# Seven products instead of eight in half the depth of 18 of the 24 tile pairs of an input projection, in split float32

## The reference, cut to what matters

```python
xn = _rmsnorm(x, n1g)
z = xn @ w_in                                  # (576, 2048) @ (2048, 6152)
bg, cg, xt, q, k, v, o, ig, fg = jnp.split(z, _SPLIT_IDX, axis=-1)
u = cg * xt
pad = jnp.concatenate([conv_buf, u], axis=1)
conv = sum(pad[:, j:j + S] * conv_w[j] for j in range(CONV_W))
y_conv = _rmsnorm(bg * conv, conv_g)
h, C1, n1, m1 = _mlstm_chunked(q, k, v, li, lf, C0, n0, m0)
y_ml = jax.nn.sigmoid(o) * _rmsnorm(h, ml_g)
x = x + jnp.concatenate([y_conv, y_ml], axis=-1) @ w_out
hn = _rmsnorm(x, n2g)
x = x + (jax.nn.silu(hn @ wg) * (hn @ wu)) @ wd
```

## Time and profile before

| | us |
|---|---|
| median of 3 runs (lowest to highest) | 2466.73 (2466.65 to 2467.93) |
| the profiled execution | 2466.16 |
| its span, first to last instruction | 2464.4 |
| TensorE busy in the span | 2444.1 |
| VectorE busy in the span | 1760.1 |
| ScalarE busy in the span | 894.7 |

### The profile page before, as it was taken

One profiled execution on the slowest core, in us unless ns is written; L12 is line 12 of the kernel. 1 busy time (PEld: TensorE's weight loads), 2 busy tenths in 40 slices (PEclk: granted clock), 3 DMA queues, 4 the chain that ended last, 5 costly groups with the idle time before them and its releaser, 6 DMA issues.

```text
span 2464.4 us, 44130 instructions
## 1 busy us (share of the span) xinstructions
PE 2444.1 (99%) x17544; PEld 2380.3 (97%) x17544; DVE 1760.1 (71%) x2453; ACT 894.7 (36%) x1235; POOL 48.3 (2%) x79
## 2 busy tenths in 40 slices
PE   9999999999999999999999999999999999999998
PEld 8999999999999998999999999999999999999886
DVE  7576585675687678778877877787777866866535
ACT  5222222122233335443344344434344533544313
POOL 0010000000000000000000000000000000000100
PEclk9999999999999999999999999999999999999999
DMA  5443343343336575443443434434334655745822
GB/s 132 118 132 89 114 120 95 85 134 95 105 101 184 174 210 174 120 120 111 128 119 104 128 111 121 118 112 121 117 101 116 246 153 160 264 129 144 286 73 77
DMA packets 459979, 329.09 MB, mean 134 GB/s; under 512 B 14407, under 2 KB 429283, under 8 KB 457425
## 3 DMA queue, kind: packets, MB, share of 16 engines
q1 hardware_dynamic: 403704, 250.29, 34.7%
q10 hardware_dynamic: 51448, 58.42, 7.6%
q0 software_dynamic: 4640, 17.73, 2.1%
HBM read 268.02 MB, written 58.37 MB: 132 GB/s over the span
## 4 chain that ended last, share of the span: by engine, by line
PE 60%; DVE 1%; ACT 0%; issue 0%; DVEq 0%; ACTq 0%
PE ps L838 17%; PE ps L842 17%; PE ps L840 17%; PE ps L853 2%; PE ps L956 2%; PE ps L958 2%; PE ps L960 2%; PE ps L983 0%; PE ps L964 0%; PE ps L965 0%; DVE oplo L2153 0%; PE ps L865 0%; DVE gw_ring L2140 0%; DVE dwlo L2409 0%; ACT ophi L1314 0%
## 5 line engine op out<-in xcount | busy, mean ns | idle before, releaser
L838 PE MATMUL ps<-ophi,gw_ring 128*128 128x288 f32 x3208 | 950.4, 296 | 5.0 <-DVE up L2197 3.5
L840 PE MATMUL ps<-oplo,gw_ring 128*128 128x288 f32 x3208 | 947.0, 295 | 0.0
L842 PE MATMUL ps<-ophi,gw_ring 128*128 128x288 f32 x3208 | 945.4, 295 | 0.0
L838 PEld LDWEIGHTS ps<-ophi,gw_ring 128*128 128x128 f32 x3208 | 602.4, 188 | 6.1 <-DVE up L2197 3.9
L842 PEld LDWEIGHTS ps<-ophi,gw_ring 128*128 128x128 f32 x3208 | 604.9, 189 | 0.0
L840 PEld LDWEIGHTS ps<-oplo,gw_ring 128*128 128x128 f32 x3208 | 603.1, 188 | 0.1
L1039 ACT ACTIVATE whi<-wraw 128x512 fp32r<-128x512 f32 x256 | 160.6, 632 | 576.2 <-PE ps L608 369.1
L605 PE MATMUL ps<-xhi,whi 128*128 128x288 f32 x1536 | 332.3, 298 | 0.5 <-DVE wlo L1612 0.5
L608 PE MATMUL ps<-xhi,wlo 128*128 128x288 f32 x1536 | 328.6, 296 | 0.0
L605 PE MATMUL ps<-xlo,whi 128*128 128x288 f32 x1536 | 328.5, 295 | 0.0
L2140 DVE TENSOR_TENSOR gw_ring<-graw_a,gw_ring 128x1024 fp32r<-128x1024 f32 x191 | 233.6, 1223 | 111.4 <-ACT gw_ring L1292 110.8
(11 more groups left out here) (339 smaller groups left out, 2669.9 us busy)
## 6 DMA issues: line engine op xcount, KB each, us to landing
wraw<-in_w_in_dram SPq DMA_DIRECT2D x96, 512.0 KB, 3.9
graw_a<-in_w_ffn_gate_dram SPq DMA_DIRECT2D x59, 512.0 KB, 3.7
graw_a<-in_w_ffn_up_dram SPq DMA_DIRECT2D x59, 512.0 KB, 4.7
graw_a<-in_w_ffn_down_dram SPq DMA_DIRECT2D x42, 512.0 KB, 5.8
wraw<-in_w_out_dram SPq DMA_DIRECT2D x32, 512.0 KB, 4.0
opraw<-hop SPq DMA_DIRECT2D x14, 1152.0 KB, 11.5
graw_b<-in_w_ffn_gate_dram SPq DMA_DIRECT2D x29, 512.0 KB, 3.8
graw_b<-in_w_ffn_up_dram SPq DMA_DIRECT2D x29, 512.0 KB, 4.7
```

What stands on the lines that cost most here:

```text
L838: pe.matmul(out, gw_ring[:, slot, 0, k, :], ophi[p][:, k, :], start=start and k == 0, stop=False, skip_group_check=True)
L840: pe.matmul(out, gw_ring[:, slot, 0, k, :], oplo[p][:, k, :], start=False, stop=False, skip_group_check=True)
L842: mm = pe.matmul(out, gw_ring[:, slot, 1, k, :], ophi[p][:, k, :], start=False, stop=k == GK - 1, skip_group_check=True)
```

## The change

Two column tiles make a pair p, six pairs a head. In 18 of the 24 pairs (head 0: pairs 3 to 5; heads 1 and 2: all; head 3: pairs 0 to 2) the k blocks 0 to 7 are computed with the seven products of the Winograd form of Strassen's method: rows of the 2 by 2 blocks are the two column tiles, the inner index is k quarter 0 or 1, the columns are the token halves. The k blocks 8 to 15 stay direct and are added into the same banks. A pair is then 11 slots of weights: seven `p` (12 matmuls each) and four `d` (24 each), 180 matmuls in place of 192. All other pairs stay direct, in slots `t` of a quarter.

Three of the seven factors of x that are sums replace or join blocks of x and are made once in head 0 (`operand_sums`, `operand_raw`, `operand_low` on VectorE, `operand_high` on ScalarE, 128 by 1152 each); the quarter of x that they replace is loaded back for head 3. The gains of the `d` and `t` slots are multiplied in by VectorE; those of the four quarters under the seven products by ScalarE (`quad_gain`, four instructions of 128 by 128). The four sums of weights are VectorE's (`weight_total`). Raw weights come in 256 KB pieces into six places. A head's outputs go to HBM (`mix_d`) and come back for the output projection, which frees the room for the new tiles. The loops over heads on SyncE, ScalarE and VectorE are written out.

```diff
+    HALF_K = ("p1", "p0", "d0", "p2", "p3", "d1", "p4", "p5", "d2", "p6", "d3")
+    seven = lambda h, p: (h == 0 and p >= 3) or 0 < h < H - 1 or (h == H - 1 and p < 3)
+            order = (("a21", "p4"), ("a22", "p6"), ("a11", "p4"), ("d0", "d0"), ("a12", "p5"), ("d1", "d1"),
+                     ("d2", "d2"), ("d3", "d3"))
...
+            def half_product(n, name, bank, start, stop, ready=None):
...
+                for k in range(4):
+                    pe.matmul(out, whi[:, w, k, :], hi[:, k, :], start=start and k == 0, stop=False, skip_group_check=True)
+                    pe.matmul(out, whi[:, w, k, :], lo[:, k, :], start=False, stop=False, skip_group_check=True)
+                    mm = pe.matmul(out, wlo[:, w, k, :], hi[:, k, :], start=False, stop=stop and k == 3,
+                                   skip_group_check=True)
+                mm.then_inc(w_used, 1)
...
+            def seven_pair(h, p, early=None, mid=None):
...
+                before = (tile_read, i + 1) if not seven(*PLAN[PLAN.index((h, p)) - 1]) else (a_read, 2 * g)
...
+                half_product(n, "p1", "c", True, False)
+                half_product(n + 1, "p0", "a", True, False, before)
+                direct_part(n + 2, 2, (("b", 0, True, False, None), ("c", 1, False, False, (copy_q, 3 * g + 1))))
+                if early:
+                    early()
...
+                half_product(n + 3, "p2", "a", False, False, (copy_q, 3 * g + 2))
+                half_product(n + 4, "p3", "b", False, False)
+                direct_part(n + 5, 3, (("b", 0, False, True, None), ("c", 1, False, False, None)))
+                if mid:
+                    mid()
...
+                half_product(n + 6, "p4", "a", False, False, (copy_q, 3 * g + 3))
+                half_product(n + 7, "p5", "c", False, True)
+                direct_part(n + 8, 2, (("d", 1, True, False, (tile_read, i + 1)), ("a", 0, False, False, (a_read, 2 * g + 1))))
...
+                half_product(n + 9, "p6", "a", False, False)
+                direct_part(n + 10, 3, (("a", 0, False, True, None), ("d", 1, False, True, None)))
...
+                if seven(h, 3):
+                    seven_pair(h, 3, mid=numerator)
+                    seven_pair(h, 4, early=sample_states)
+                    head_squares()
+                    seven_pair(h, 5)
+                    seven_pair(h + 1, 0)
...
+            def quad_gain(h, p, name):
...
+                for k in range(4):
+                    ins = act.mul(raw_slot[j][:, k, :], raw_slot[j][:, k, :], vecs[:, col + k:col + k + 1])
+                ins.then_inc(quad_ok, 1)
...
+                n = FIRST[h, p] + s + 4
...
+                hi(n)
+                h, p, name = SLOTS[n]
+                if seven(h, p) and name in ("p1", "d0"):
+                    quad_gain(h, p, dict(p1="a11", d0="a12")[name])
+                elif name in ("p6", "d3", "t12", "t13"):
+                    nxt = PLAN[PLAN.index((h, p)) + 1:][:1]
+                    if nxt and seven(*nxt[0]):
+                        quad_gain(*nxt[0], "a21" if name in ("p6", "t12") else "a22")
...
+            def ahead(n):
+
+                if n < N_IN:
+                    h, p, s = SLOTS[n]
+                    if by_vector(s):
+                        gain(n)
+                    elif s in SUMS:
+                        weight_total(h, p, s)
+
+            def split(n):
+
+                ahead(n + 1)
+                low(n)
...
+                def c11(h, p, out):
+                    g = SEVENTH[h, p]
+                    slot_done(slot_of(h, p, "d1"))
+                    dve.wait_ge(copy_q, 3 * g + 2)
+                    link(tt(p1s[:], ps[:, 2, 0:HT], p1s[:], ALU.add))
+                    return out(p1s[:], 0)
...
+                def c21_c22(h, p, out):
+                    g = SEVENTH[h, p]
+                    slot_done(slot_of(h, p, "d3"))
+                    out(ps[:, 0, 0:HT], 0).then_inc(a_read, 1)
+                    dve.wait_ge(a_read, 2 * g + 1)
+                    link(tt(p5s[:], ps[:, 1, 0:HT], p5s[:], ALU.add))
+                    evac(out(p5s[:], 1))
...
+                    step(h, 5, 0)
+                    rms_of_h()
+                    step(h, 5, 1)
+                    rms_rest()
+                    sum_squares(0)
+                    steps(h, 5, 2, 3, 4, 5)
+                    link(c11(h, 5, by_tile(cg, cg)))
+                    conv_prompt(0, HT)
+                    u3(h, 5)
+                    step(h, 5, 6)
+                    mixed_heads()
+                    step(h, 5, 7)
+                    c12(h, 5, by_tile(cg, cg))
+                    dve.wait_ge(tile_read, i + (10 + 2))
+                    conv_prompt(HT, T)
+                    step(h, 5, 8)
+                    conv_sample(1)
+                    conv_scaled(1)
+                    step(h, 5, 9)
+                    c21_c22(h, 5, by_tile(own_conv(1), cv))
+                    step(h, 5, 10)
```

More of the change, by code:

```diff
@@ L380, in _, with load_out @@
         def _(sp):
[L381 to L390, removed]
+            def load_out(m, p, before):
+                for half in range(2):
+                    sp.wait_ge(lo_done, before(half))
+                    sp.sem_inc(halves_free, 1)
+                    sp.dma_start(wraw[:, half, 0:8, :], w_out_k[:, ds(MIX_K[8 * half], 8), ds(m * P + p * (GK * P), P)]).then_inc(raw_in[half], 16)
             xp = x_prompt.rearrange("l t d -> (l t) d")
@@ L399, in _, with load_quarter @@
                 sp.dma_start(xtok[last:XTW, XT - 1, c], xs[:, c]).then_inc(tok_in[b], 16)
[L401 to L410, removed]
+            def load_quarter(h, p, name, j, free):
+                if free:
+                    sp.wait_ge(lo_done, free)
+                k0 = 4 * quarter_k(h, p, name)
+                sp.dma_start(raw_slot[j], w_in_k[:, k0:k0 + 4, ds(column_of(h, p, name), P)]).then_inc(g_raw[j], 16)
             def small_inputs():
@@ new lines, in gemm @@
+                for n in range(KT):
+                    w = ring(n0 + n // 4)
+                    if n % 4 == 0:
+                        pe.wait_ge(lo_done, n0 + n // 4 + 1)
+                    if n in between:
+                        between[n]()
+                    if ready:
+                        ready(n)
+                    k, (out, first, last) = ks[n], where[n]
+                    for moving in (hi, lo):
+                        for a in halves:
+                            pe.matmul(out[:, a, :], whi[:, w, n % 4, :], moving[:, 2 * k + a, :],
+                                      start=first and moving is hi, stop=False)
+                    for a in halves:
+                        mm = pe.matmul(out[:, a, :], wlo[:, w, n % 4, :], hi[:, 2 * k + a, :],
+                                       start=False, stop=last)
+                    if n % 4 == 3:
+                        mm.then_inc(w_used, 1)
@@ L2011, in round_of_head @@
[L2011 removed]
+                step(h, 5, 7)
+                sum_squares(1)
+                rows_from_psum()
             def mix_low(n):
@@ L2024, in rows_from_psum @@
                 dve.tensor_copy(conv_rows[:], side(BLK_B, DC)[0:2 + 2 * NB]).then_inc(rows_out, 1)
[L2026 to L2031 removed]
+            for h in range(H):
+                round_of_head(h)
             for n in range(10, KT):
```

1244 lines of the change are left out of this document (795 added, 449 removed).

## The result

| us | before | after |
|---|---|---|
| median of 12 runs each, taken side by side (lowest to highest) | 2466.88 (2466.06 to 2468.39) | 2471.93 (2469.71 to 2475.36) |
| the profiled execution | 2466.16 | 2471.64 |
| its span | 2464.4 | 2469.8 |
| mean granted clock of TensorE in it | 0.998 | 0.995 |

The ratio is 1.0021, with a 95% interval of 1.0013 to 1.0028. The forecast was 2463.5, a gain of 0.13%; the time came out 8.4 us above it, inside the range of 2443 to 2481.

The account below looks back on a forecast made before the run. TensorE, busy for 99% of the span, was taken as the bound. 2466.16 less 28.8 for removed matmuls plus 25.5 of stalls gave 2462.9; with 0.57 for the median of runs, 2463.5 us, range 2443 to 2481.

Parts of the forecast that it names:

- pairs 0, 1, 2: Light pairs of a head: VectorE's 15 us and at most 3.5 us of head pieces fit, no stall.
- `p0` behind pair 3: TensorE waits for VectorE's `c21` to free bank 0 after pair 3: 1.0 us a head.
- `d2` of pair 4: VectorE splits slot 8 late in pair 4: 1.4 us, then 0.9 to 1.0 at its second half; 2.4 us lost.
- the transfers, at `d3` of pair 4: ScalarE's `quad_gain` waits for a weight piece in pair 4, delaying `d3`: 1 us a head, bounds 0 and 4.
- `p0` behind pair 5: VectorE frees bank 0 at 29.7 us, TensorE wants it at 25.6 after the heaviest pair: 4.1 us lost a head.
- the sum: Stalls of 8.5 us a head over three heads, 25.5 us, set against 28.8 us of removed matmuls: 2462.9 us.
- the clock falls: TensorE's clock drops after the stall behind pair 5, thrice: 5.3 us more, 2469 us; chance 0.18.
- The gain comes through: VectorE's pieces fit in pairs 3 to 5, only 0 to 2 us a head lost: 2441 us; chance 0.24.
- ScalarE stands in line for a transfer: `quad_gain` waits ahead of `d3`'s rounding in pairs 4 and 5: 7.2 us a head more, 2485 us; chance 0.18.

Follow-up runs that it names:

- experiment 1: Changed kernel with VectorE's mixed outputs made in pair 0 of the next head instead of pair 5: 2457.1 us, ratio to before 0.9961.
- 12: Changed kernel with mixed outputs in next pair 0, spills tied to pair 5's `c12`, `sample_update` behind pair 4's `u3`, three gains a head by ScalarE: 2443.9 us.
- experiment 5: Changed kernel with 36 TensorE transposes of a constant filling each wait behind pair 5, computation unchanged: 2467.6 us, ratio to before 1.0001.
- experiment 7: Changed kernel with mixed outputs in the next pair 0 and GpSimd's spread and spill waiting for them: 2470.6 us, ratio to before 1.0014.
- experiment 3: Changed kernel with GpSimd's spread and spill after the next head's mixed outputs, in pair 5 instead of pair 4: 2467.0 us, ratio to before 0.9998.

## Why the prediction was wrong

**The working that held.** 216 matmuls at 0.133 us went. The steps beside what they measured, each for a head:

| step | forecast | measured in heads 0, 1, 2 |
|---|---|---|
| pairs 0, 1, 2 | no stall | none |
| `p0` behind pair 3 | 1.0 | 1.07 |
| `d2` of pair 4 | 1.4 + 1.0 | 1.87 + 0.57 |
| the transfers, at `d3` of pair 4 | 1.0 | 0, 1.12, 1.11 |
| `p0` behind pair 5 | 4.1 | 3.91, 3.95, 3.97 |
| second half of `d2` in pair 5 | none | 0, 0.33, 0.33 |

The three heads sum to 25.5 forecast and 25.2 measured. A sum of instructions in one queue, with its slots' ends beside it, foresaw VectorE's waits to within half a microsecond; the term for the transfers was 1.0 off in head 0. Most instructions cost what their nearest rows did. VectorE's timeline of after ahead of the end of the long wait shows the piece that experiment 1 moved, and the read that frees the bank:

```profile
373.28 0.81 DVE L2307 SCALAR_TENSOR_TENSOR v0f<-v0f,gml,rh 128x576 f32<-128x576 f32 x1
...
383.80 0.45 DVE L2109 TENSOR_TENSOR mixf<-ps,cv 128x288 f32<-128x288 f32 x1
```

Part of the closeness is luck, because errors cancel. The mixed outputs take 3.05 us, not 3.7: the row's 356.51 to 360.23 holds idle time, 0.35 of it shown there. VectorE came to pair 5 0.9 us later than forecast (3.0 us into it), and TensorE asked for the bank 0.8 us later (at 26.4). In pair 4 one subtraction took 1.92 us instead of 0.69, in each of the three heads, beside GpSimd's addition for the root mean square. VectorE's timeline and GpSimd's in head 1:

```profile
335.27 1.92 DVE L1881 TENSOR_TENSOR wlo<-wraw,whi 128x512 fp32r<-128x512 f32 x1
...
334.74 1.90 POOL L1842 TENSOR_TENSOR kf<-kf,qf 128x576 f32<-128x576 f32 x1 [34.16 <-ACT qf L1357]
```

GpSimd's addition too was longer than the 1.43 us that it takes in before, where it stands beside VectorE's update of the states (329.52 us). These 1.2 us of VectorE are in the first wait at `d2` and in no term of mine; TensorE came to `d2` 0.9 us later than forecast and the second wait there was 0.4 shorter, so that the sum of the two, 2.44 against 2.4, shows nothing of them. No experiment took them away.

**The step that failed** is the sum, 2466.16 - 28.8 + 25.5: it prices a stall at its idle time alone. The rival "the clock falls", to which I gave 0.18, was to have been part of the likeliest case, since the forecast had the stall of 4.1 us that its condition asks for. It was priced at 5.3 us and measured at 5.1 in the profiled execution, and experiment 5, whose edit removes nothing but the idle there, gave back 4.4 in the median. Of the rival's time, 2469, the measured 2471.9 is 3 us off. Against it stand the 2.6 us of the start to start count and the 1.8 of the second matmuls, 0.28 us for each of 16 waits, and the later beginning of 0.6, none of which had a term; what is not placed has the other sign. The reason that I gave against it, that TensorE was half idle around the place in the earlier trace rows and full here, counted for nothing: TensorE was full up to the stall, and the clock fell all the same, 1.4 us after its end in head 0 and before its end in heads 1 and 2. The Trainium skill (TensorE: Matmul & The Clock Gate, "Why this matters for your kernels") warns of idle gaps between bursts of matmuls, and the profile of after agrees: three gaps of 3.9 us, three falls to the lower level, 48 matmuls at 0.24 us. The page would not have led me to expect the falls behind 1.86 us that experiment 5's profile shows.

**The other rivals.** "The gain comes through" needed pieces that overlap, and they don't as written; but 12 comes to 2443.9 near its 2441, through the order of work, the place of the transfers and three gains a head given to ScalarE. "ScalarE stands in line for a transfer" has its mechanism in the profile, ScalarE's 3.70 and 2.03 us in front of its gains, but at the size that the forecast took (1.1 us at `d3`, in two of three heads), not the 4.6. In experiment 7, in a pair 0, ScalarE's gain stands for 7.66 us in front of a transfer, but VectorE's own gain stands there as long (7.75), so it is not ScalarE's queue alone that holds TensorE.

**Open.** About 0.7 us of the account, and 0.5 behind the input projection, are not placed. Whether the second half of pair 5's `d2` is late through the same burst was only made likely by experiment 3, where it goes with the `d3` wait. Why the clock falls behind some waits of 1.9 us and not behind others is open: 5 of 21 is a count over one execution of each kernel. That GpSimd's addition is what stretches the subtraction rests on the two standing side by side in all three heads; no run separates them.

## What to carry to other kernels

Price a stall on TensorE as its idle time, plus what its end costs (0.23 to 0.27 us here at the full clock), plus the slow matmuls behind it (1.1 to 2.6 us here after 3.9 us of idle). By these prices a stall of 3.9 us costs about 5 to 7 us. When work is taken from the bound engine, go through the next engine's order around each short-lived buffer: a piece whose result nobody needs soon is to stand behind the read that frees the buffer, and this was worth 14.8 us here, half of what the change removed. Move a piece on one engine only after asking whose cover its partner on the other engine was, and tie a burst of transfers to a point of the schedule that later edits don't move.

## What was unexpected in the hardware

- A wait costs TensorE more than the idle time that the profile shows: 4.08 us lost from start to start against 3.91 shown, and 27.8 against 25.2 over 16 waits. The step behind it is longer too, 0.21 to 0.24 us instead of 0.133.
- The fall of the clock is not tied to the long waits alone: at a wait of 1.86 us it was 0.71 in the window in experiment 5's profile (some 13 matmuls at 0.24 us from 172.2), and 1.00 in after's at the same wait; over all profiles 5 of 21 such waits had a fall behind them, and 12 of 12 of 3.9 to 4.0 us. In after, behind the same 3.9 us, it lasted for 14, 24 and 10 matmuls.
- A transpose of 128 by 128 takes 0.11 us at the full clock (17 in 2.02 us, 36 in 4.09), about as much as a matmul of 288 columns with 0.133. 36 of them in a wait held the clock at 1.00 all three times.
- A VectorE subtraction of 128 by 512 took 1.92 us instead of 0.69 beside a GpSimd addition of 128 by 576, which itself took 1.90 instead of 1.43.
